# Softmax sums: scaling the probabilities before they are turned instead of the attended values after

## What is computed

```python
# group A
scores = jnp.where(valid, q @ k * hd ** -0.5 + bias, NEG_INF)
probs = jax.nn.softmax(jnp.concatenate([scores, sink_col], axis=-1), axis=-1)[..., :-1]
out_a = probs @ v
# group D
p = jax.nn.softmax(q @ k * hd ** -0.5, axis=-1)
out_d = p @ v
# both
mix = concatenate([rms_norm(o, g) for o in (out_a, out_b, out_c, out_d)])
h = layer_norm(DN_ALPHA * h + mix @ w_out, ln1_g, ln1_b)
```

## Time and profile before

| | |
|---|---|
| median of 3 runs | 1061.21 us (1061.2 to 1061.98) |
| the profiled execution | 1062.26 us |
| its span in the profile | 1059.8 us |
| PE busy | 1044.2 us, 99% |
| DVE busy | 774.9 us, 73% |
| ACT busy | 538.8 us, 51% |
| POOL busy | 117.2 us, 11% |

### The profile page before, as it was taken

One profiled execution on the slowest core, in us unless ns is written; L12 is line 12 of the kernel. 1 busy time (PEld: TensorE's weight loads), 2 busy tenths in 40 slices (PEclk: granted clock), 3 DMA queues, 4 the chain that ended last, 5 costly groups with the idle time before them and its releaser, 6 DMA issues.

```text
span 1059.8 us, 15245 instructions
## 1 busy us (share of the span) xinstructions
PE 1044.2 (99%) x5281; PEld 868.3 (82%) x5281; DVE 774.9 (73%) x1075; ACT 538.8 (51%) x809; POOL 117.2 (11%) x122
## 2 busy tenths in 40 slices
PE   8999999999999999999999999999999999999997
PEld 6888887888888888888888888879888888888885
DVE  7845886868658757758887568777884784785687
ACT  3433666565265355355634247656634643652654
POOL 5200243200000000000002004331000000000003
PEclk9999999999999999999999999999999999999999
DMA  8432023031521521431333410211243134125122
GB/s 290 161 119 80 1 61 121 9 120 43 196 80 40 196 81 39 164 114 46 114 140 143 159 41 21 108 53 49 80 136 142 40 109 169 40 84 193 40 80 80
DMA packets 17378, 105.47 MB, mean 100 GB/s; under 512 B 2016, under 2 KB 2704, under 8 KB 5792
## 3 DMA queue, kind: packets, MB, share of 16 engines
q1 hardware_dynamic: 15984, 98.70, 26.0%
q0 software_dynamic: 1184, 5.86, 1.7%
q10 hardware_dynamic: 144, 0.07, 0.0%
HBM read 101.49 MB, written 2.10 MB: 98 GB/s over the span
## 4 chain that ended last, share of the span: by engine, by line
PE 93%; DVE 2%; issue 1%; POOL 1%; DMA 1%; ACT 1%; DVEq 0%; SPq 0%; POOLq 0%; ACTq 0%
PE bank L466 18%; PE bank L467 18%; PE bank L468 18%; PE bank L814 9%; PE bank L815 9%; PE bank L813 9%; PE bank L754 2%; PE bank L739 1%; PE bank L475 1%; PE bank L645 1%; PE bank L646 1%; DVE mx L1562 1%; DMA x<-in_x 1%; PE bank L542 1%; POOL x L1922 1%
## 5 line engine op out<-in xcount | busy, mean ns | idle before, releaser
L466 PE MATMUL bank<-h_hi,w_hi 128*128 128x512 f32 (+1 forms) x688 | 257.8, 375 | 0.0
L467 PE MATMUL bank<-h_lo,w_hi 128*128 128x512 f32 (+1 forms) x688 | 257.5, 374 | 0.0
L468 PE MATMUL bank<-h_hi,w_lo 128*128 128x512 f32 (+1 forms) x688 | 257.4, 374 | 0.0
L813 PE MATMUL bank<-w_hi,hid_hi 128*128 128x512 f32 x448 | 174.4, 389 | 0.0
L815 PE MATMUL bank<-w_hi,hid_lo 128*128 128x512 f32 x448 | 174.3, 389 | 0.0
L814 PE MATMUL bank<-w_lo,hid_hi 128*128 128x512 f32 x448 | 174.3, 389 | 0.0
L1259 DVE TENSOR_TENSOR w_lo<-w_raw,w_hi 128x2048 fp32r<-128x2048 f32 x62 | 141.9, 2288 | 39.2 <-ACT w_hi L929 32.7
L929 ACT CAST w_hi<-w_raw 128x2048 fp32r<-128x2048 f32 x56 | 107.2, 1914 | 85.3 <-PE bank L815 61.5
L467 PEld LDWEIGHTS bank<-h_lo,w_hi 128*128 128x128 f32 x688 | 129.6, 188 | 23.2
L466 PEld LDWEIGHTS bank<-h_hi,w_hi 128*128 128x128 f32 x688 | 129.5, 188 | 23.2
L468 PEld LDWEIGHTS bank<-h_hi,w_lo 128*128 128x128 f32 x688 | 129.5, 188 | 22.8
(11 more groups left out here) (183 smaller groups left out, 1632.1 us busy)
## 6 DMA issues: line engine op xcount, KB each, us to landing
w_raw<-in_weights SPq DMA_DIRECT2D x63, 1024.0 KB, 4.8
w_third<-in_weights SPq DMA_DIRECT2D x23, 1024.0 KB, 4.8
rows<-in_rows POOLq DMA_DIRECT2D x4, 1024.0 KB, 5.0
w_raw<-in_weights SPq DMA_DIRECT2D x4, 512.0 KB, 9.1
out_h<-x SPq DMA_DIRECT2D x8, 256.0 KB, 2.0
x<-in_x SPq DMA_DIRECT2D x3, 512.0 KB, 10.8
dft<-in_dft SPq DMA_DIRECT2D x2, 512.0 KB, 7.2
qk_gain<-in_qk_gain POOLq DMA_DIRECT2D x3, 192.0 KB, 3.3
```

The lines of the kernel that those rows point to most:

```text
L466: pe.matmul(dst, s_hi, m_hi, start=first, stop=False)
L467: pe.matmul(dst, s_hi, m_lo, start=False, stop=False)
L468: return pe.matmul(dst, s_lo, m_hi, start=False, stop=last)
L813: pe.matmul(bank[dst + t][:], s_hi, m_hi, start=start, stop=False, skip_group_check=goes_on)
```

## The change

The probabilities are divided by their sum before they are turned. DVE inverts two sums per pair (`invert_pair`), POOL multiplies both units' tiles in `stage` in place (`scale_probs`), and `turn_probs` waits for that (`scaled`). `head_out`, the widened inverse, its transposes and its copy are gone; squares, `mix_hi` and `mix_lo` read the values' bank directly. In A the sink's logit is put as one more column into `stage`, so that maximum and sum take it in. The reduction negates by itself, and D's factor goes into the copy of `dq`. `pT` has four places instead of two, and values of both pairs of a quad are taken together in odd steps, the quad's sum in the even step that follows. POOL's queue is written by steps. The sides 0 and 1 behind step 15 move ahead of the turning of pair 15.

The diff, cut to its core, with its indentation shortened:

```diff
-def quad_scaled_in(step):
+def quad_high_in(step):
     return (step - 3) // 2 if step >= 3 and step % 2 else None
...
-def quad_inverted_in(step):
-    return quad_scaled_in(step + 1)
-def quad_high_in(step):
-    return quad_scaled_in(step - 1)
+def quad_low_in(step):
+    return quad_high_in(step - 1)
...
 def quad_mean_in(step):
-    return quad_scaled_in(step - 2)
+    return quad_high_in(step - 2)
...
 dk_lo = share("dk_lo", [P, 2, SEQ], F32R)
-pT = share("pT", [P, 2, BANK])
+pT_even = share("pT_even", [P, 2, BANK])
 y, at_y = place("y", [P, 2, SEQ])
...
+pT_odd, _ = place("pT_odd", [P, 2, BANK], F32, at=rest[0])
+pT = (pT_even, pT_odd)
 folded = share("folded", [P, TOK, GROUP])
...
-src = head_out[:, q % 2, :].rearrange("p (c n) -> p c n", c=2)
+src = bank[4 + q % 2][:, 0:GROUP].rearrange("p (c n) -> p c n", c=2)
 g, t = 2 + q // 4, q % 4
...
-    def turn_inverse(q):
-        wait(pe, l, "inv_widened", q + 1)
-        for j in range(2):
-            last = pe.transpose(bank[4 + q % 2][:, GROUP + j * P:GROUP + (j + 1) * P], inv_wide[:, j * P:(j + 1) * P], ident)
-        last.then_inc(sems["inv_turned"], 1)
     def sum_quad(q):
...
         wait(pe, l, "out_square_added", q + 1)
+        wait(pe, l, "mix_lo", 2 + q + 1)
         pe.matmul(bank[4 + q % 2][:, GROUP:GROUP + 1], head_square[:, 0:P], ones[:], start=True, stop=True)\
...
         _, _, _, _, k0, k1 = unit(u)
-        wait(pe, l, "probs", u + 1)
+        wait(pe, l, "scaled", u + 1)
         if u >= 2:
...
                 v = dv[:, k0 + i, d] if in_d else tk[:, k0 + i, 2 * P + kv * HEAD_DIM:2 * P + (kv + 1) * HEAD_DIM]
-                done = pe.matmul(bank[4 + (p // 2) % 2][d, j * P:(j + 1) * P], v, pT[:, kv, i * P:(i + 1) * P],
+                done = pe.matmul(bank[4 + (p // 2) % 2][d, j * P:(j + 1) * P], v, pT[p % 2][:, kv, i * P:(i + 1) * P],
                                  start=(i == 0), stop=(i == k1 - k0 - 1))
...
             side(k)
-        if p >= 2:
+        if p >= 3 and p % 2:
+            take_values(p - 3)
             take_values(p - 2)
-        if quad_scaled_in(p) is not None:
-            turn_inverse(quad_scaled_in(p))
-        if quad_high_in(p) is not None:
-            sum_quad(quad_high_in(p))
+        if quad_low_in(p) is not None:
+            sum_quad(quad_low_in(p))
         for u in pair(p - 1):
...
     take_values(PAIRS - 2)
+    last_sides = list(sides_of(PAIRS))
+    side(last_sides[0])
+    side(last_sides[1])
     for u in pair(PAIRS - 1):
...
     sum_quad(6)
     turn_half(l, 1, 0, 1)
     take_values(PAIRS - 1)
-    turn_inverse(7)
-    last_sides = list(sides_of(PAIRS))
-    side(last_sides[0])
-    side(last_sides[1])
-    sum_quad(7)
     turn_stream(1)
+    sum_quad(7)
     side(last_sides[2])
...
         wait(act, l, "qk_turned", 2 + j + 1)
-        act.copy(dq[:, j, :], bank[j][:]).then_inc(sems["dq_copied"], 1)
+        act.activation(dq[:, j, :], bank[j][:], ACT.Copy, scale=HEAD_DIM ** -0.5).then_inc(sems["dq_copied"], 1)
...
-    def copy_inverse(q):
-        wait(act, l, "inv_turned", q + 1)
-        if q >= 1:
-            wait(act, l, "head_out", q)
-        act.copy(inv_rows[:], bank[4 + q % 2][:, GROUP:]).then_inc(sems["inv_copied"], 1)
     def square_head_out(q):
-        wait(act, l, "head_out", q + 1)
+        wait(act, l, "attended", 4 * q + 4)
         if q >= 1:
             wait(act, l, "quad_sum", q)
-        act.activation(head_square[:], head_out[:, q % 2, :], ACT.Square).then_inc(sems["out_square"], 1)
+        act.activation(head_square[:], bank[4 + q % 2][:, 0:GROUP], ACT.Square).then_inc(sems["out_square"], 1)
...
         wait(act, l, "prob_turned", u + 1)
-        if u >= 2:
-            wait(act, l, "attended", u - 1)
-        act.copy(pT[:, u % 2, 0:(k1 - k0) * P], bank[2 + u % 2][:, 0:(k1 - k0) * P]).then_inc(sems["prob_copied"], 1)
+        if u >= 4:
+            wait(act, l, "attended", u - 3)
+        act.copy(pT[(u // 2) % 2][:, u % 2, 0:(k1 - k0) * P], bank[2 + u % 2][:, 0:(k1 - k0) * P]).then_inc(sems["prob_copied"], 1)
...
     for p in range(PAIRS):
-        if quad_high_in(p) is not None:
-            square_head_out(quad_high_in(p))
         for u in pair(p):
...
         if quad_high_in(p) is not None:
+            square_head_out(quad_high_in(p))
             mix_high_quad(quad_high_in(p))
-        if quad_scaled_in(p) is not None:
-            copy_inverse(quad_scaled_in(p))
         for u in pair(p - 1):
...
             split_half(13, p - 9, 32)
-    square_head_out(6)
-    mix_high_quad(6)
     for u in pair(PAIRS - 1):
         copy_turned(u)
-    copy_inverse(7)
     stream_high_tile(0)
...
-    wait(act, l, "head_out", 8)
-    mix_high_quad(7)
     square_head_out(7)
+    mix_high_quad(7)
     stream_high_tile(1)
...
-    def invert_quad(q):
+    def invert_pair(p):
-        b = q % 2
-        wait(dve, l, "probs", 4 * q + 4)
-        if q >= 2:
-            wait(dve, l, "inv_widened", q - 1)
-        total = p_sum[:, b, :]
-        if q < 4:
-            dve.tensor_tensor(den[:, b, :], p_sum[:, b, :], sink_e[:, b, :], ALU.add).then_inc(sems["denom"], 1)
-            wait(dve, l, "denom", q + 1)
-            total = den[:, b, :]
-        dve.reciprocal(inv[:, b, :], total).then_inc(sems["inv_denom"], 1)
-    def scale_quad(q):
-        b = q % 2
-        wait(dve, l, "attended", 4 * q + 4)
-        wait(dve, l, "inv_copied", q + 1)
-        if q >= 2:
-            wait(dve, l, "out_square", q - 1)
-        dve.tensor_tensor(head_out[:, b, :], bank[4 + b][:, 0:GROUP], inv_rows[:], ALU.mult).then_inc(sems["head_out"], 1)
+        b, i = (p // 2) % 2, 2 * (p % 2)
+        wait(dve, l, "probs", 2 * p + 2)
+        if p >= 4:
+            wait(dve, l, "scaled", 2 * (p - 4) + 2)
+        dve.reciprocal(inv[:, b, i:i + 2], p_sum[:, b, i:i + 2]).then_inc(sems["inv_denom"], 1)
...
             d0 = (k0 - qb + 1) * P
+            dve.tensor_copy(stage[:, u % STAGES, n:n + 1], cols[:, COL_SINK + head:COL_SINK + head + 1]).then_inc(sems["sink_put"], 1)
             dve.scalar_tensor_tensor(out=stage[:, u % STAGES, 0:n], in0=dist[:, d0:d0 + n], scalar=2.0 ** (-8.0 * (head + 1) / A_HEADS),
                                      in1=bank[u % 2][:, 0:n], op0=ALU.mult, op1=ALU.add).then_inc(sems["biased"], 1)
+            wait(dve, l, "sink_put", u + 1)
             wait(dve, l, "biased", u + 1)
-            dve.reduce_max(mx[:, sl], stage[:, u % STAGES, 0:n], AX_X).then_inc(sems["row_max"], 1)
-            wait(dve, l, "row_max", u + 1)
-            dve.tensor_scalar(neg_mx[:, sl], mx[:, sl], cols[:, COL_SINK + head:COL_SINK + head + 1], -1.0,
-                              ALU.max, ALU.mult).then_inc(sems["neg_max"], 1)
+            dve.tensor_reduce(neg_mx[:, sl], stage[:, u % STAGES, 0:n + 1], AX_X, ALU.max, negate=True).then_inc(sems["neg_max"], 1)
         else:
-            dve.reduce_max(mx[:, sl], bank[u % 2][:, 0:n], AX_X).then_inc(sems["row_max"], 1)
-            wait(dve, l, "row_max", u + 1)
-            dve.tensor_scalar(neg_mx[:, sl], mx[:, sl], -HEAD_DIM ** -0.5, None, ALU.mult).then_inc(sems["neg_max"], 1)
+            dve.tensor_reduce(neg_mx[:, sl], bank[u % 2][:, 0:n], AX_X, ALU.max, negate=True).then_inc(sems["neg_max"], 1)
...
     for p in range(PAIRS):
+        if quad_low_in(p) is not None:
+            mix_low_quad(quad_low_in(p))
         if quad_mean_in(p) is not None:
...
                 side(k)
-        if quad_high_in(p) is not None:
-            mix_low_quad(quad_high_in(p))
-        if quad_inverted_in(p) is not None:
-            invert_quad(quad_inverted_in(p))
-        if quad_scaled_in(p) is not None:
-            scale_quad(quad_scaled_in(p))
+        if p < PAIRS - 1:
+            invert_pair(p)
         if p in (4, 6):
...
             normalise_first(l, 0)
-    invert_quad(7)
     mix_low_quad(6)
+    invert_pair(PAIRS - 1)
     normalise_first(l, 1)
     mean_quad(6)
-    scale_quad(7)
     stream_low(l, 1, 0)
...
         pool.tensor_tensor(sqg[:, 0, :], sqg[:, 0, :], sqg[:, 1, :], ALU.add).then_inc(sems["square_added"], 1)
-        if g == 1:
-            for j in range(2):
-                wait(pool, l, "mix_hi", 2 + j + 1)
-                pool.tensor_tensor(mix_lo[:, 2 + j, :], co[:, j, :], mix_hi[:, 2 + j, :].bitcast(F32), ALU.subtract)\
-                    .then_inc(sems["fourier_lo"], 1)
+    def group_power(g):
         wait(pool, l, "square_mean", g + 1)
...
+    def fourier_low(j):
+        wait(pool, l, "mix_hi", 2 + j + 1)
+        pool.tensor_tensor(mix_lo[:, 2 + j, :], co[:, j, :], mix_hi[:, 2 + j, :].bitcast(F32), ALU.subtract)\
+            .then_inc(sems["fourier_lo"], 1)
     def dq_low(j):
...
-    def widen_inverse(q):
+    def scale_probs(u):
-        wait(pool, l, "inv_denom", q + 1)
-        if q >= 1:
-            wait(pool, l, "inv_turned", q)
-        pool.tensor_copy(inv_wide[:].rearrange("p (h d) -> p h d", h=4),
```

(56 more changed lines are left out.)

20 lines of the change are left out of this document (4 added, 16 removed).

## The result

The changed kernel takes **1088.99 us** (median of 4 runs, 1087.92 to 1091.03), the kernel before 1061.2: ratio 1.0263, 95% interval [1.0247, 1.0278]. The prediction was 1063.9, with a range of 1060 to 1071. The direction was right, the loss is 28 us instead of 3, and the time lies outside the range.

The account below looks back on a forecast made before the run. PE was taken as the bound, busy 1044.2 of 1059.8 us. Per layer -3.65 + 4.0 + 1.0 = +1.35, twice 2.7 us, giving a median of 1063.9 us; range 1060 to 1071.

Parts of the forecast that it names:

- What PE loses: PE's attention part: removed transposes save 1.9 us and merged value batches 1.75 us, together -3.65 us per layer.
- even: Tail behind step 15: neither gain nor loss, plus or minus 1 us, its removed transposes counted as lost.
- What is free: DVE and ACT in the attention part: shorter queues and small added operations cost nothing, covered by slack within a step.
- What POOL gains: POOL multiplies 32 tiles per layer in place: 0.75 us per 512 columns, ends 0.62 and 1.29.
- The new stop: PE waits at the quad's sum for POOL's addition: 4.0 us in step 12, 1.0 in step 14, per layer.
- rival (3): POOL's multiply costs as much as a two-tensor operation, 1.29 us: 1072 us in all; chance 10%.
- one of the prediction's own signs of being wrong: PE's attention part: a stop of PE in steps 1 to 10 would show the prediction wrong.
- rival (5): Clock falls during the 4 us stop, step 13 runs at 1.2 GHz: 6.65 us more per layer, 1077; chance 2%.
- A lock beside it: POOL's multiply meets DVE's SBUF operations: over a step of slack in steps 4, 6, 14; up to 1 us in tail.
- Rival (4): Sink copies into `stage` wait behind POOL's multiplies and delay the maxima: twice 2 us, 1068; chance 5%.
- Rivals (1): Cheap POOL multiply of 0.62 us per tile and mild tail: 1061 up to 1063.3, same time; chance 34%.
- (2): Step 12: POOL's addition is there in time, PE is not held: 1054 to 1058, faster; chance 13%.

Follow-up runs that it names:

- kernel 1: The changed kernel with no multiply anywhere, the turning waiting for the exponentials alone: 1053.99 us, ratio 0.9927 to the kernel before.
- 4: The changed kernel with each POOL multiply covering only 47 of every 128 columns of its tile: 1066.42 us, ratio 1.0047 to the kernel before.
- 6: The changed kernel with every POOL multiply as a two-tensor operation, the inverse sum broadcast along the row: 1070.22 us, ratio 1.0086 to the kernel before.
- 5: The changed kernel with POOL's multiply by a constant 1.0 in even units and as a two-tensor operation in odd units: 1075.8 us, ratio 1.0141.
- kernel 9: The changed kernel with the multiply of the probabilities moved from POOL to DVE, behind the reciprocal: 1064.68 us, ratio 1.0031 to the kernel before.

## Why the prediction was wrong

| kernel | multiply, 512 columns | stops in steps 10, 12, 14 | time over kernel 1 |
|---|---|---|---|
| prediction | 0.75 | 0, 4.0, 1.0 | |
| 4 | 0.75 | 0, 3.66, 1.05 | 12.4 |
| 6 | 1.03 | 0.64, 4.16, 1.56 | 16.2 |
| 5 | 1.50 and 1.03 | 1.58, 4.62, 2.03 | 21.8 |
| the change | 1.55 | 2.83, 5.25, 3.01 | 35.0 |

**What PE loses**: right within 0.3 us. -3.65 per layer was predicted, kernel 1 shows -3.8. The agreement is partly luck, since the parts were off against each other: merging 1.3 instead of 1.75, the rest 2.5 instead of 1.9. The second contains the tail, where the stops went from 0.58 and 0.67 to 0.37 and 0.77, so "even" was right.

**What is free**: right as long as nothing is put on DVE; kernel 9 shows how little of its slack can be used.

**What POOL gains**: this step failed. The price was taken "near the copy, since only one tensor is read"; 0.75 against 1.55 measured. The upper bound failed as well: that a one-tensor operation cannot cost more than the two-tensor addition (1.29) was an assumption that no row showed. Put into the prediction's own formulas, 1.55 gives 4.0 + 1.6 = 5.6 in step 12 (measured 5.25), 1.0 + 1.6 = 2.6 in step 14 (3.01) and 4 x 0.8 - 0.2 = 3.0 in step 10 (2.83). **The new stop**, its places, its releaser and the four multiplies in front of step 10 were thus right, and rival (3), the dearer multiply, was the right mechanism at too low a price, with 10%. The stops in steps 4 and 6 (0.17 and 0.84) were in no sum, and PE stopping in steps 1 to 10 was one of the prediction's own signs of being wrong. Five stops per layer of 12.1 less 3.8 of savings leave 8.3. The Trainium skill (GPSIMD Engine Reference, Elementwise side-by-side) gives 769 ns as a best case for 512 elements; POOL took twice that or more in every D tile (1.55, and 2.16 in the pair of step 15).

**The clock**: rival (5) was given 2% on the strength of one wait of 4.4 us in the first 20 us, behind which the granted clock was 1.00. In the change stops of 2.83 to 5.25 us were enough. Part of (5) came true, at a smaller price than its 6.65: 1.6 to 2.7 behind five of the six stops of steps 10, 12 and 14, 9.9 us in all. The Trainium skill (TensorE: Matmul & The Clock Gate, Part 1) says that the clock halves after idleness; here the traces agree: matmuls of 512 columns start 0.43 apart behind the stops instead of 0.23.

The evidence against (5) was also misread. PE's timeline before, behind that wait and later:

```profile
4.37 3.67 PE L516 MATMUL bank<-ident_first 128*128 128x128 f32 x16 [4.37 <-DMA ident_first<-in_ident_first]
7.83 0.42 PE L510 MATMUL bank<-ident_first 128*128 128x128 f32 x1
...
15.62 1.03 PE L475 MATMUL bank<-ident_first,x 128*128 128x128 f32 x8
16.41 0.71 PE L549 MATMUL bank<-w_lo,h_hi 128*128 128x512 f32 x2
```

Sixteen transposes of 128 columns take 3.46 us behind the wait, 0.22 each; eight take 0.79 later, 0.10 each. The eight of L475 are recorded with 1.66 at 8.13 us, and with 1.03 at 15.62. In the change they take 0.20 each at the lower level (1.60 for eight, at 178.09) and 0.10 at the higher. So PE ran at the lower pace behind the 4.4 us wait too, and the 1.00 of the clock column in that first stretch is not borne out by the rows. Of the 28 us, 8.3 x 2 = 16.6 are the sum with the right price, 9.9 the clock, and 1.3 are not assigned.

**A lock beside it** came where it was expected. POOL's pair took 3.42 instead of 2.48 in step 4 (384 columns), 2.78 instead of 1.83 in step 6 (256), and 3.75 and 4.32 instead of 3.1 in steps 14 and 15. But "over a step of slack" was not so: the long pair of step 4 stands in POOL's queue ahead of the addition for which L716 stopped 0.84 us in step 6, and its 0.94 more is enough to account for that stop. The 0.17 in step 4 came before it. In step 14 the addition itself took 0.80 instead of 0.45, beside VectorE's normalising, which is most of the 0.4 between 3.01 and 2.6. Rival (4) did not occur: no wait of PE goes back to the sink copies. Rivals (1) and (2) needed a multiply of under 0.66, and a split that began early; neither was so.

What stays open: why POOL's operation with one tensor is slower than the one with two. Nor is it known why the same stop cost clock in one layer and not in the other (2.83 us in the change, 1.44 and 0.57 in kernel 9), or what holds PE in the gaps of steps 12 and 14 of kernel 1.

## What to carry to other kernels

Where the trace has no row for an operation, the nearest row with the same number of inputs is no bound, neither is one with more of them. An in-order engine that gains work on the path has to be summed over several steps, with everything queued between two points at which the bottleneck meets it, since moving one item can merely move the stop. Work that waits on a reciprocal belongs to the engine with slack that does not get held by another's instructions. A stop of PE can also cost clock on top of its length, and the same stop need not do so each time: here 1.6 on 3.01, 2.4 and 2.7 on 5.25, and 0 or 1.6 on 2.83. And a clock figure is to be checked against the pace of the rows beside it.
